# A two-layer float32 backbone kernel: 22 seven-product pairs instead of 20, and sums made by accumulating transfers

## The chip, the core and the metric

The kernel runs on one core of a Trainium2 chip. The metric is the device time of one execution in microseconds (us). Five engines work side by side, each through its own list of instructions in order: PE (TensorE, matmuls), DVE (VectorE), ACT (ScalarE), POOL (GpSimd) and SP (SyncE). They wait for each other by semaphores. SP and POOL issue the transfers between the chip's memory (HBM) and the on-chip memory (SBUF); PE writes its sums to PSUM, which has eight banks of 512 columns.

## The reference

Two layers over 256 latent tokens and 256 context tokens, 1024 channels, all in float32. Each layer is a feed-forward, a mixer (attention, gated convolution, pooling) and a second feed-forward. Only the latent tokens are returned, so the last feed-forward works on them alone, and three feed-forwards work on 512 tokens.

```python
D_MODEL, SEQ, CTX_LEN, D_FF, N_MOD = 1024, 256, 256, 2816, 9
def _swiglu(x, w_gu, w_down):
    g, u = jnp.split(x @ w_gu, 2, axis=-1)
    return (jax.nn.silu(g) * u) @ w_down
...
for l in range(DEPTH):
    mod = (silu_c @ w_mod[l] + b_mod[l]).reshape(B, N_MOD, D_MODEL)
    mod_c = (silu_cc @ w_mod[l] + b_mod[l]).reshape(1, N_MOD, D_MODEL)
    h = h + 0.5 * m[2][:, None] * _swiglu(_modulate(_rms(h, norm_w[l, 0]), m[0], m[1]), ...)
    hc = hc + 0.5 * mc[2][:, None] * _swiglu(...)
    y, yc = _hybrid_mixer(u, uc, ctx_out, w_in[l], w_out[l], ...)
    h = h + m[5][:, None] * y
    h = h + 0.5 * m[8][:, None] * _swiglu(...)
    if ctx_out:
        hc = ...
return h
```

## The kernel before, in words

Activations lie with channels on the 128 partitions and the 512 tokens (latent, context) along the columns: `h` is [128, 8 chunks, 512]. Weights come as a stream of 320 blocks of 128 x 1024 numbers (512 KB) through a ring `raw` of five slots. SP loads block n once PE has finished block n-5.

**Products in three parts.** To keep float32 accuracy, each number is split into a high part (rounded to the fast format) and a low part (the rest). ACT makes `whi` (the high part of a block, line 546), DVE makes `wlo` (the block minus `whi`, line 980). The activations have `xh` and `xl` in the same way, and the hidden values `ah` and `al`. A product is three matmuls: high weight by high x, high weight by low x, low weight by high x (lines 1699 to 1701). An ordinary block is 8 chunks of 3 matmuls of 512 columns.

**A feed-forward** has 22 pairs of blocks (gate and up, pair j writes 128 hidden channels to `hid`) and 22 blocks of the down projection. At pair j, PE waits for the hidden product of pair j-2. ACT applies silu to the gate, DVE multiplies (`hidden`, line 1011). The feed-forwards are numbered f = 0 (layer 0, first), 1 (layer 0, second), 2 (layer 1, first) and 3 (the last, of another form).

**Seven-product pairs.** For the pairs in `SEVENS[f]`, the gate and up blocks are taken as a 2 x 2 matrix of halves and multiplied with the halves of x by the Winograd form of Strassen's scheme: seven products of half size (4 chunks, 3 matmuls each, 256 columns: 84 matmuls) instead of eight (48 matmuls of 512 columns). It needs four sums of halves of x, made once per feed-forward (`x_whole`, `x_sums`, `x_sums_low`: from `xh + xl` = `x32`, which lies in `hid`, to `t32`, then `thi` and `tlo`), and three sums of halves of the weights per pair (`weight_sums` to `s32`, then `shi` and `slo`). One of the seven products needs up-half + gate-half itself, which DVE writes in place into the up block in `raw` (line 1067), before ACT splits that block. PE's third product waits for all of `tlo`, its fifth for `slo`. DVE combines the products (`seven_begin`, `seven_end`, `seven_mul`).

**Modulation.** `modc` = c times `w_mod`, for latent and context. DVE makes it in between: a "pair" is one load of 512 KB into `wm` and two multiply-and-sum operations of 1024 columns, one per stream (`mod_pair`, line 998). There are 36 units of four pairs. POOL loads `wm`, two buffers in turn, one load after each `wm_used` (line 501). How many pairs DVE makes in which step is set by two tables: `MODS_GU[f]` (by pair of blocks) and `MODS_DN[f]` (by block of the down projection); `UNIT_AT[f]` is the first unit and their number.

**The order** of each engine's work is what the loops of `ffn` on DVE, ACT and PE write out; nothing is reordered later. In DVE's loop a step j makes, in this order: splits for pair j+2, or sums and splits of the next seven-product pair; work on x; modulation pairs; the hidden product of j; more splits. `seven(f, j)` decides the branch.

Of the kernel before, what the change touches and what calls it, by code (L numbers as in the profile page):

```python
# [26 lines left out]
P = 128  # L27
D = 1024
DC = D // P
# [53 lines left out]
MODS_GU = ({2: 1, 3: 1, 4: 2, 5: 2, 7: 2, 8: 2, 9: 2, 11: 2, 12: 2, 13: 2, 15: 2, 16: 2, 17: 2, 19: 2, 20: 2, 21: 1},  # L83
           {1: 1, 2: 1, 3: 1, 5: 2, 7: 2, 9: 2, 11: 2, 13: 2, 15: 2, 17: 2, 19: 2, 20: 2, 21: 1},
           {1: 1, 2: 1, 3: 1, 5: 2, 7: 2, 9: 2, 11: 2, 13: 2, 15: 2, 17: 2, 19: 2, 20: 2, 21: 1})
MODS_DN = ({b: 1 for b in range(18)} | {12: 2}, {b: 1 for b in range(18)} | {12: 2, 13: 2, 14: 2, 15: 2},
           {b: 1 for b in range(14)})
HALVES_AT = {20: (0, 1), 21: (2, 3, 4)}
# [27 lines left out]
def program(nc, wstream, wmod, cols, x_t, out):  # L116
    with ExitStack() as ctx:
# [208 lines left out]
        xn_lo = sem("xn_lo")  # L326
        x_sum = sem("x_sum")
        tsum_done = sem("tsum_done")
        thi_done = sem("thi_done")
        tlo_done = sem("tlo_done")  # L330
        wsum_done = sem("wsum_done")
# [8 lines left out]
        silu_a = sem("silu_a")  # L340
# [94 lines left out]

        def seventh(f, j):
            return sum(len(SEVENS[i]) for i in range(f)) + SEVENS[f].index(j)
# [51 lines left out]
        @block.gpsimd  # L489
        def _(pool):  # L490
            u0 = START_UNITS * PAIRS
            pool.wait_ge(wm0_in[DC - 1], 16)
            for c in range(2):
                pool.dma_start(wm[:, c, :, :].rearrange("p a n -> p (a n)"), wmod[u0 + c]).then_inc(wm_in[c], 16)

            def loads(a, b):
                with pool.Fori(a, b) as i:
                    for c in range(2):

                        pool.wait_ge(wm_used, i * 2 + (c - 1 - u0))  # L500
                        pool.dma_start(wm[:, c, :, :].rearrange("p a n -> p (a n)"),  # L501
                                       wmod[bass.ds(i * 2 + c, 1)].rearrange("a p n -> p (a n)"))\
                            .then_inc(wm_in[c], 16)
# [23 lines left out]
            after_mix = (LATE_UNIT + 1) * PAIRS // 2 + 1  # L527
            loads(u0 // 2 + 1, after_mix)
            zeros(0)
            conv_pool_low(0)  # L530
            loads(after_mix, UNITS * PAIRS // 2)
            zeros(1)
            conv_pool_low(1)
# [3 lines left out]
        def _(act):  # L537
# [38 lines left out]
            def weight_sums_high(f, j, n):  # L576

                k = seventh(f, j)
                split(n)
                act.wait_ge(wsum_done, 4 * k + 2)  # L580
                split(n + 1)
                act.wait_ge(wsum_done, 4 * k + 4)
                act.activation(shi[:, :, :, :].rearrange("p k c n -> p (k c n)"),
                               s32[:, :, :].rearrange("p k n -> p (k n)"), ACT.Copy).then_inc(shi_done, 1)

            def silu_seven(f, j):

# [3 lines left out]
                act.activation(ups[:, 0:S], ps[:, 7, 0:S], ACT.Copy).then_inc(s1_done, 1)  # L591
                act.wait_ge(gate_a, k + 1)
                act.activation(sil[:, j % 2, 0:S], first_up[:, 0:S], ACT.Silu).then_inc(silu_a, 1)  # L593
                act.wait_ge(gate_b, k + 1)
                act.activation(sil[:, j % 2, S:T], first_up[:, S:T], ACT.Silu).then_inc(silu_done, 1)

            def ffn(l, st):
# [4 lines left out]
                for j in range(FC):  # L602
# [11 lines left out]
                    if j == 3:  # L614
                        x_sums_high()
                    for c in HALVES_AT.get(j, ()):
# [351 lines left out]
        def _(dve):  # L968
            steps = [0]
# [18 lines left out]
            def mod_pair(u, p, junk=products):  # L988
# [6 lines left out]
                for v in range(2):  # L995
# [3 lines left out]
                                             accum_out=flat[:, at:at + 1]).then_inc(mod_acc, 1)  # L999
# [24 lines left out]
            def x_whole():  # L1024

                for c in range(0, DC, 2):
                    dve.tensor_tensor(x32[:, c:c + 2, :, :, :].rearrange("p c s h t -> p (c s h t)"),
                                      xh32[:, c:c + 2, :].rearrange("p c t -> p (c t)"),
                                      xl[:, c:c + 2, :].bitcast(F32).rearrange("p c t -> p (c t)"), ALU.add)\
                        .then_inc(x_sum, 1)  # L1030

            def x_sums(g):
# [8 lines left out]
                dve.wait_ge(x_sum, 4 * g + 4)  # L1041
# [15 lines left out]
            def weight_sums(f, j, n):  # L1057
# [4 lines left out]
                dve.wait_ge(raw_in[(n + 1) % RING], 16 * ((n + 1) // RING + 1))  # L1062
                if k:
                    dve.wait_ge(products43, k)
                h = KQ * P
                dve.tensor_tensor(s32[:, 0, :], up[:, 0:h], up[:, h:2 * h], ALU.add).then_inc(wsum_done, 1)
# [34 lines left out]
            def seven_end(f, j):  # L1101
# [6 lines left out]
                dve.tensor_tensor(pair_of(ups), twice(two_ups[:, 0:S]), last, ALU.add).then_inc(ups_done, 1)  # L1108

            def seven_mul(f, j):  # L1110
# [3 lines left out]
                halves = hid[:, j * T:(j + 1) * T].rearrange("p (s h t) -> p s h t", s=2, h=2)  # L1114
                for i in range(2):
                    if i:
                        dve.wait_ge(silu_done, FC * f + j + 1)
                    else:
                        dve.wait_ge(silu_a, k + 1)
                    ins = dve.scalar_tensor_tensor(halves[:, :, i, :],  # L1120
                                                   ups[:, i * S:(i + 1) * S].rearrange("p (s t) -> p s t", s=2), -1.0,
                                                   sil[:, j % 2, i * S:(i + 1) * S].rearrange("p (s t) -> p s t", s=2),
                                                   ALU.mult, ALU.mult)
                ins.then_inc(mul_done, 1)
# [113 lines left out]
            def ffn(l, st):  # L1238
# [13 lines left out]
                for j in range(FC):  # L1252
# [14 lines left out]
                    if j == 3:  # L1267
                        x_sums_low(f)
                    for c in HALVES_AT.get(j, ()):
# [1059 lines left out]
```

## Time and profile before

| | |
|---|---|
| time, median of three runs | 1630.32 us (1627.26 to 1631.6) |
| profiled execution | 1629.36 us, of which the span of instructions is 1627.7 |
| PE busy | 1612.9 us (99%), mean granted clock 0.999 |
| DVE busy | 1272.3 us (78%) |
| ACT busy | 690.1 us (42%) |
| POOL busy | 84.7 us (5%) |
| moved by transfers | 250.46 MB, mean 154 GB/s |

The profile is one execution with a row per instruction. A row's idle time stands before it, with what ended it behind an arrow. Matmuls overlap: each row's duration includes its pipeline's depth, so the distance from start to start is the price of one, and a PE that shows as busy may still be spaced out. "Granted clock" is the share of TensorE's full clock.

### The profile page before, as it was taken

What the parts mean: (1) busy time and instruction counts of PE and PEld (TensorE: products, weight loads), DVE (VectorE), ACT (ScalarE), POOL (GpSimd) and SP (SyncE); (2) the same over time, 40 slices, a digit from 0 to 9 for tenths busy, and PEclk for the clock granted to TensorE, in tenths of its full rate; (3) what the DMA queues carried; (4) which work ended last, traced back from release to release, by engine and by line L of the source; (5) the groups of instructions that cost most, each with busy time, mean ns of one, the idle gap of its engine ahead of it and who ended that gap; (6) DMA issues with size and microseconds to landing.
All of it is one profiled execution on the core that took longest, in us unless ns stands there. A gap on an engine that the chain in (4) does not pass through costs nothing.

```text
span 1627.7 us, 24207 instructions
## 1 busy us (share of the span) xinstructions
PE 1612.9 (99%) x9396; PEld 1404.6 (86%) x9396; DVE 1272.3 (78%) x1973; ACT 690.1 (42%) x1056; POOL 84.7 (5%) x149
## 2 busy tenths in 40 slices
PE   8999999999999999999999899999999999999999
PEld 4888888889878898999888798999888997999888
DVE  5887777887878679888878889888888487877654
ACT  5422233324856453333343153333333275665542
POOL 0000000110000100000000100000000000100000
PEclk9999999999999999999999999999999999999999
DMA  9454455563321224444455634444455232365554
GB/s 380 148 191 172 168 174 163 195 200 100 113 67 52 79 97 155 150 147 151 155 176 187 206 105 160 150 147 149 155 179 182 95 114 83 103 201 188 183 187 149
DMA packets 69613, 250.46 MB, mean 154 GB/s; under 512 B 7552, under 2 KB 8576, under 8 KB 69376
## 3 DMA queue, kind: packets, MB, share of 16 engines
q1 hardware_dynamic: 51072, 181.84, 33.3%
q0 software_dynamic: 18432, 67.12, 12.8%
q8 instruction: 74, 1.21, 0.3%
q14 instruction: 35, 0.29, 0.1%
HBM read 247.88 MB, written 1.05 MB: 153 GB/s over the span
## 4 chain that ended last, share of the span: by engine, by line
PE 92%; DVE 5%; DMA 2%; issue 1%; ACT 1%; DVEq 0%; POOLq 0%; ACTq 0%
PE ps L1699 27%; PE ps L1700 26%; PE ps L1701 26%; PE ps L1742 3%; PE ps L1790 2%; PE ps L1743 2%; DMA wm<-wmod 1%; PE ps L1792 1%; PE ps L2108 1%; PE ps L1851 1%; PE ps L2076 1%; DVE shared_b L998 1%; DVE wm L998 1%; DVE wlo L980 1%; PE ps L2090 0%
## 5 line engine op out<-in xcount | busy, mean ns | idle before, releaser
L980 DVE TENSOR_TENSOR wlo<-raw,whi 128x1024 fp32r<-128x1024 f32 x320 | 387.5, 1223 | 191.7 <-ACT whi L546 188.9
L1699 PE MATMUL ps<-xh,whi 128*128 128x512 f32 (+1 forms) x1420 | 497.1, 350 | 2.7 <-DVE xl L1185 2.3
L1700 PE MATMUL ps<-xl,whi 128*128 128x512 f32 (+1 forms) x1420 | 489.1, 344 | 0.0
L1701 PE MATMUL ps<-xh,wlo 128*128 128x512 f32 (+1 forms) x1420 | 488.8, 344 | 0.0
L546 ACT ACTIVATE whi<-raw 128x1024 fp32r<-128x1024 f32 x320 | 335.6, 1056 | 354.6 <-PE ps L1701 269.1
L1699 PEld LDWEIGHTS ps<-xh,whi 128*128 128x128 f32 x1420 | 268.7, 189 | 41.2 <-DVE xl L1185 4.4
L1701 PEld LDWEIGHTS ps<-xh,wlo 128*128 128x128 f32 x1420 | 268.7, 189 | 32.6
L1700 PEld LDWEIGHTS ps<-xl,whi 128*128 128x128 f32 x1420 | 268.9, 189 | 32.3 <-issue 0.7
L1700 PE MATMUL ps<-al,whi 128*128 128x512 f32 (+2 forms) x768 | 263.8, 343 | 0.0
L1699 PE MATMUL ps<-ah,whi 128*128 128x512 f32 (+1 forms) x668 | 236.2, 354 | 4.7 <-DVE wlo L980 2.8
L1701 PE MATMUL ps<-ah,wlo 128*128 128x512 f32 (+1 forms) x668 | 235.5, 353 | 0.0
L1700 PEld LDWEIGHTS ps<-al,whi 128*128 128x128 f32 x768 | 146.3, 190 | 17.1
L998 DVE SCALAR_TENSOR_TENSOR wm<-wm,cb 128x1024 f32<-128x1024 f32 x128 | 156.1, 1220 | 0.0
L1699 PEld LDWEIGHTS ps<-ah,whi 128*128 128x128 f32 x668 | 126.9, 190 | 23.1 <-DVE wlo L980 3.0
L1701 PEld LDWEIGHTS ps<-ah,wlo 128*128 128x128 f32 x668 | 126.9, 190 | 16.9
L501 POOL DMA_DIRECT2D wm<-wmod x126 | 66.6, 529 | 983.6 <-DVEq L1001 959.0
L559 ACT ACTIVATE shared_b<-ps 128x512 f32<-128x512 f32 x46 | 27.5, 599 | 208.8 <-PE ps L1701 208.7
L998 DVE SCALAR_TENSOR_TENSOR shared_a<-wm,cb 128x1024 f32<-128x1024 f32 x73 | 89.1, 1221 | 10.2 <-DMA wm<-wmod 5.7
L1011 DVE TENSOR_TENSOR hid<-shared_b,ps 128x512 f32<-128x512 f32 x46 | 31.6, 687 | 69.5 <-ACT shared_b L559 66.7
L998 DVE SCALAR_TENSOR_TENSOR shared_b<-wm,cb 128x1024 f32<-128x1024 f32 x55 | 67.0, 1219 | 8.8 <-DMA wm<-wmod 8.7
L1742 PE MATMUL ps<-xh,whi 128*128 128x512 f32 x208 | 73.5, 399 | 0.0
L593 ACT ACTIVATE shared_b<-shared_b 128x256 f32<-128x256 f32 x20 | 8.4, 419 | 137.5 <-DVE shared_b L1094 137.5
(217 smaller groups left out, 2295.6 us busy)
## 6 DMA issues: line engine op xcount, KB each, us to landing
raw<-wstream SPq DMA_DIRECT2D x320, 512.0 KB, 3.5
wm<-wmod POOLq DMA_DIRECT2D x128, 512.0 KB, 4.8
wm<-wmod SPq DMA_DIRECT2D x8, 1024.0 KB, 16.8
h<-x_t SPq DMA_DIRECT2D x4, 512.0 KB, 6.4
cb<-cols SPq DMA_DIRECT2D x1, 1024.0 KB, 19.7
out_t<-h SPq DMA_DIRECT2D x8, 128.0 KB, 2.6
K<-cols SPq DMA_DIRECT2D x1, 907.0 KB, 19.9
K<-cols SPq DMA_DIRECT2D x1, 265.5 KB, 2.9
```

The lines of the kernel that those rows point to most:

```text
L501: pool.dma_start(wm[:, c, :, :].rearrange("p a n -> p (a n)"), wmod[bass.ds(i * 2 + c, 1)].rearrange("a p n -> p (a n)"))\
L546: act.activation(whi[:, n % SPL, :, :].rearrange("p a b -> p (a b)"), raw[:, n % RING, :], ACT.Copy)\
L559: act.activation(sil[:, j % 2, 0:w], ps[:, gu_bank(f, 2 * j), 0:w], ACT.Silu).then_inc(silu_done, 1)
L980: dve.tensor_tensor(wlo[:, n % RING, :, :].rearrange("p a b -> p (a b)"), raw[:, n % RING, :], whi[:, n % SPL, :, :].rearrange("p a b -> p ...
L998: dve.scalar_tensor_tensor(rows if v else junk, rows, 1.0, cb[:, v, :], ALU.mult, ALU.mult, accum_out=flat[:, at:at + 1]).then_inc(mod_acc, 1)
L1011: dve.tensor_tensor(hid[:, j * T:j * T + w], sil[:, j % 2, 0:w], ps[:, gu_bank(f, 2 * j + 1), 0:w], ALU.mult).then_inc(mul_done, 1)
L1699: pe.matmul(out_ap, hi_w, hi_x, start=start, stop=False)
L1700: pe.matmul(out_ap, hi_w, lo_x, start=False, stop=False)
L1701: return pe.matmul(out_ap, lo_w, hi_x, start=False, stop=stop)
L1742: pe.matmul(ps[:, bank, :], whi[:, n % SPL, c, :], xh[:, c, :], start=c == 0, stop=False)
L1743: return pe.matmul(ps[:, bank, 0:S], wlo[:, n % RING, c, :], xh[:, c, 0:S], start=False, stop=c == DC - 1)
L1790: pe.matmul(ps[:, banks[d], 0:2 * w], hi_w, pair.rearrange("p v t -> p (v t)"), start=start, stop=False)
```

## The change

- `SEVENS`: in feed-forwards 1 and 2 the seven-product pairs are now the even ones from 4 to 20 (nine each) instead of the odd ones from 5 to 19 (eight each). Feed-forward 0 keeps its four.
- Whole x: DVE's four additions go. POOL copies `xh` into `x32` with two transfers of 1 MB (SBUF to SBUF), waits for both, and adds `xl` to it with two accumulating transfers (`accum_op`). DVE's `x_sums` stands at step 4 of feed-forward 0 and step 2 of the others, and waits for `x_sum`.
- Weight sums in feed-forwards 1 and 2: POOL adds half of the gate block from HBM onto the up block in `raw` (256 KB, accumulating, `third_sum`); DVE then makes three sums instead of four. DVE's sums and ACT's split of that block wait for `third_in`.
- `seven_mul`: one operation of 512 columns instead of two of 256; ACT's silu writes its halves in the order of the tokens.
- Modulation: from unit 28 on (`X_ONLY`) only the latent stream's operation is made, the context's columns are set to zero once. The pairs are dealt anew: 48, 36 and 44 in feed-forwards 0 to 2 instead of 48, 44 and 36.
- POOL's loads are written out in order, between the other transfers, instead of a loop.
- `HALVES_AT`: in feed-forwards 1 and 2 the first five hidden splits all stand at step 21.

```diff
-UNIT_AT = {0: (4, 12), 1: (16, 11), 2: (27, 9)}
+UNIT_AT = {0: (4, 12), 1: (16, 9), 2: (25, 11)}
+X_ONLY = 28
+X_SUMS_AT = (4, 2, 2)
+ACCUMULATED = (1, 2)
-SEVENS = ((7, 11, 15, 19), (5, 7, 9, 11, 13, 15, 17, 19), (5, 7, 9, 11, 13, 15, 17, 19))
+SEVENS = ((7, 11, 15, 19),
+          (4, 6, 8, 10, 12, 14, 16, 18, 20),
+          (4, 6, 8, 10, 12, 14, 16, 18, 20))
...
-MODS_DN = ({b: 1 for b in range(18)} | {12: 2}, {b: 1 for b in range(18)} | {12: 2, 13: 2, 14: 2, 15: 2},
-           {b: 1 for b in range(14)})
...
+             {21: (0, 1, 2, 3, 4)},
...
+            def whole_x(f):
+
+                if f == 0:
+                    pool.wait_ge(mul_done, 1)
+                pool.wait_ge(xl_done, XT[(0, 2, 3)[f]] + 2 * DC)
+                for c in (0, KQ):
+                    pool.dma_start(x32[:, c:c + KQ, :, :, :].rearrange("p c s h t -> p (c s h t)"),
+                                   xh32[:, c:c + KQ, :].rearrange("p c t -> p (c t)")).then_inc(x_copy, 16)
+                pool.wait_ge(x_copy, 32 * (f + 1))
+                for c in (0, KQ):
+                    pool.dma_start(x32[:, c:c + KQ, :, :, :].rearrange("p c s h t -> p (c s h t)"),
+                                   xl[:, c:c + KQ, :].bitcast(F32).rearrange("p c t -> p (c t)"), accum_op=ALU.add)\
+                        .then_inc(x_sum, 16)
+
+            def third_sum(f, j):
+
+                n = first_block(f) + 2 * j + 1
+                pool.wait_ge(raw_in[n % RING], 16 * (n // RING + 1))
+                pool.dma_start(raw[:, n % RING, 0:KQ * P], wstream[n - 1][:, 0:KQ * P], accum_op=ALU.add)\
+                    .then_inc(third_in, 16)
+
+            def ffn(f, m0):
+
+                made = m0
+                if f:
+                    whole_x(f)
+                for j in range(FC):
+                    if f == 0 and j == 1:
+                        whole_x(f)
+                    made += MODS_GU[f].get(j, 0)
+                    loads_to(u0 + 2 + made)
+                    if f in ACCUMULATED and seven(f, j + 2):
+                        third_sum(f, j + 2)
+                loads_to(u0 + 2 + made + sum(MODS_DN[f].values()))
+                return made + sum(MODS_DN[f].values())
...
-                act.wait_ge(wsum_done, 4 * k + 2)
+                if f in ACCUMULATED:
+                    act.wait_ge(third_in, 16 * (k - before_accumulated + 1))
+                else:
+                    act.wait_ge(wsum_done, 4 * k + 2)
...
-                    if j == 3:
+                    if j == X_SUMS_AT[f] + 1:
                         x_sums_high()
...
-                for v in range(2):
+                for v in range(2 if u < X_ONLY else 1):
...
-            def x_whole():
-
-                for c in range(0, DC, 2):
-                    dve.tensor_tensor(x32[:, c:c + 2, :, :, :].rearrange("p c s h t -> p (c s h t)"),
...
-                dve.wait_ge(x_sum, 4 * g + 4)
+                dve.wait_ge(x_sum, 32 * (g + 1))
...
+                if f in ACCUMULATED:
+                    dve.tensor_tensor(s32[:, 1, :], up[:, 0:h], up[:, h:2 * h], ALU.add).then_inc(wsum_done, 2)
+                    dve.wait_ge(wsum_done, 4 * k + 2)
+                    dve.tensor_tensor(s32[:, 0, :], s32[:, 1, :], gate[:, 0:h], ALU.subtract).then_inc(wsum_done, 1)
+                    dve.tensor_tensor(s32[:, 2, :], s32[:, 1, :], gate[:, h:2 * h], ALU.add).then_inc(wsum_done, 1)
+                    return
...
-                    if j == 1:
-                        x_whole()
-                    if j == 2:
+                    if j == X_SUMS_AT[f]:
                         x_sums(f)
```

How the instructions move. DVE, start of feed-forward 1, before, from the first hidden products on (`t<-hid` are the token sums, `tlo<-t,thi` their low parts, `s<-raw` the first weight sum, `wm,modc` a modulation operation):

```order
L1042 TENSOR_TENSOR t<-hid 128x1024 [waits x_sum]
L1043 TENSOR_TENSOR t<-hid 128x1024
L1045 SCALAR_TENSOR_TENSOR t<-t,hid 128x1024 [waits tsum_done]
L1048 SCALAR_TENSOR_TENSOR t<-t,hid 128x1024 [waits tsum_done]
L998 SCALAR_TENSOR_TENSOR shared_a,modc<-wm,cb 128x1024 [waits wm_in1]
L998 SCALAR_TENSOR_TENSOR wm,modc<-wm,cb 128x1024
L1011 TENSOR_TENSOR hid<-shared_b,ps 128x512 [waits mod_acc,silu_done]
L980 TENSOR_TENSOR wlo<-raw,whi 128x1024 [waits hi_done]
L1054 TENSOR_TENSOR tlo<-t,thi 128x1024 [waits thi_done] x4
```

and after:

```order
L1093 TENSOR_TENSOR t<-hid 128x1024 [waits x_sum]
L1094 TENSOR_TENSOR t<-hid 128x1024
L1096 SCALAR_TENSOR_TENSOR t<-t,hid 128x1024 [waits tsum_done]
L1099 SCALAR_TENSOR_TENSOR t<-t,hid 128x1024 [waits tsum_done]
L1070 TENSOR_TENSOR hid<-shared_b,ps 128x512 [waits silu_done]
L1121 TENSOR_TENSOR s<-raw 128x512 [waits third_in,products43,raw_in2]
L1123 TENSOR_TENSOR s<-s,raw 128x512 [waits wsum_done]
L1124 TENSOR_TENSOR s<-s,raw 128x512
L1038 TENSOR_TENSOR wlo<-raw,whi 128x1024 [waits hi_done,wsum_done]
L1038 TENSOR_TENSOR wlo<-raw,whi 128x1024 [waits hi_done]
L1136 TENSOR_TENSOR slo<-s,shi 128x1536 [waits shi_done]
L1105 TENSOR_TENSOR tlo<-t,thi 128x1024 [waits thi_done] x4
```

The modulation operations have gone from here, and the weight sums of the first seven-product pair now stand between the token sums and their low parts, a pair earlier than before.

POOL at the same place, after (before, only loads of `wm` stood here, each waiting for `wm_used`); `hid<-xh` and `hid<-xl` are the transfers of whole x, `raw<-wstream` the third sums:

```order
L526 DMA hid<-xh 128x2048 [waits xl_done]
L526 DMA hid<-xh 128x2048
L530 DMA hid<-xl 128x2048 [waits x_copy]
L530 DMA hid<-xl 128x2048
L538 DMA raw<-wstream 128x512 [waits raw_in3]
L538 DMA raw<-wstream 128x512 [waits raw_in2]
L517 DMA wm<-wmod 128x1024 [waits wm_used] x2
L538 DMA raw<-wstream 128x512 [waits raw_in1]
```

The third sum of the first seven-product pair stands behind all four transfers of whole x in POOL's list.

## Rows read from the trace of the kernel before

**Rows 1.** The page, busy time of each engine.
```profile
PE 1612.9 (99%) x9396; PEld 1404.6 (86%) x9396; DVE 1272.3 (78%) x1973; ACT 690.1 (42%) x1056; POOL 84.7 (5%) x149
```
**Rows 2.** Waits of PE: total us, times, longest.
```profile
PE ps L1699 <- DVE wlo L980: 3.0, 2, 2.8
PE ps L1699 <- DVE xl L1185: 2.3, 4, 0.6
PE ps L1699 <- DVE h L1135: 1.9, 1, 1.9
```
**Rows 3.** Timeline of PE, pairs 4 and 5, feed-forward 1: start, duration, instruction.
```profile
629.98 0.39 PE L1699 MATMUL ps<-xh,whi 128*128 128x512 f32 x1
...
640.86 0.28 PE L1699 MATMUL ps<-xh,whi 128*128 128x256 f32 x1
...
650.93 0.40 PE L1699 MATMUL ps<-xh,whi 128*128 128x512 f32 x1
```
**Rows 4.** Timeline of PE, end of feed-forward 1; idle in brackets.
```profile
923.13 0.28 PE L1701 MATMUL ps<-ah,wlo 128*128 128x256 f32 x1
926.20 0.39 PE L1699 MATMUL ps<-ah,whi 128*128 128x256 f32 x1 [2.79 <-DVE wlo L980]
...
933.42 0.28 PE L1701 MATMUL ps<-ah,wlo 128*128 128x256 f32 x1
935.62 0.39 PE L1699 MATMUL ps<-ah,whi 128*128 128x256 f32 x1 [1.92 <-DVE h L1135]
```
**Rows 5.** Busy by window: PE, PEld, DVE, ACT, POOL; clock, DMA share, GB/s.
```profile
927.00:935.00 8.00, 6.70 (x44) 6.50 (x42) 7.71 (x17) 0.00 (x0) 1.06 (x2) 0.79 0.42 144
```
**Rows 6.** Timeline of DVE, end of feed-forward 1, two splits in succession.
```profile
917.37 1.23 DVE L980 TENSOR_TENSOR wlo<-raw,whi 128x1024 fp32r<-128x1024 f32 x1
...
924.92 1.23 DVE L980 TENSOR_TENSOR wlo<-raw,whi 128x1024 fp32r<-128x1024 f32 x1
```
**Rows 7.** Timeline of DVE, start of feed-forward 1.
```profile
597.08 1.27 DVE L1185 SCALAR_TENSOR_TENSOR xl<-shared_b,modc,xh 128x256 fp32r<-128x256 f32 x3
...
616.70 1.22 DVE L1042 TENSOR_TENSOR t<-hid 128x1024 f32<-128x1024 f32 x1
...
620.23 1.23 DVE L1048 SCALAR_TENSOR_TENSOR t<-t,hid 128x1024 f32<-128x1024 f32 x1
...
625.63 4.62 DVE L1054 TENSOR_TENSOR tlo<-t,thi 128x1024 fp32r<-128x1024 f32 x4
...
635.94 2.36 DVE L980 TENSOR_TENSOR wlo<-raw,whi 128x1024 fp32r<-128x1024 f32 x2
638.22 1.75 DVE L1076 TENSOR_TENSOR slo<-s,shi 128x1536 fp32r<-128x1536 f32 x1
```
**Rows 8.** Timeline of DVE, feed-forward 0, hidden products of pairs 0 and 3.
```profile
50.11 0.69 DVE L1011 TENSOR_TENSOR hid<-shared_b,ps 128x512 f32<-128x512 f32 x1 [0.68 <-ACT shared_b L559]
...
81.85 0.69 DVE L1011 TENSOR_TENSOR hid<-shared_b,ps 128x512 f32<-128x512 f32 x1
```
**Rows 9.** Landings of `raw`, of `wm`; transfers, 0:40 (two rows), then 598:618.
```profile
DMA to landing us min/median/max: 3.3/3.5/18.2
...
DMA to landing us min/median/max: 3.6/4.8/19.3
...
GB/s 0 19 212 364 363 356 326 348 412 428 410 426 410 418 422 410 401 414 414 410 401 414 414 410 401 410 422 406 406 397 418 401 406 418 439 396 388 403 438 389
...
q1 hardware_dynamic: 4469, 15.03, 96.3%
...
q1 hardware_dynamic: 720, 2.62, 37.7%
```
**Rows 10.** Groups of DVE by form: busy us, mean ns, idle before.
```profile
L998 DVE SCALAR_TENSOR_TENSOR wm<-wm,cb 128x1024 f32<-128x1024 f32 x128 | 156.1, 1220 | 0.0
L1011 DVE TENSOR_TENSOR hid<-shared_b,ps 128x512 f32<-128x512 f32 x46 | 31.6, 687 | 69.5 <-ACT shared_b L559 66.7
L1066 DVE TENSOR_TENSOR s<-raw 128x512 f32<-128x512 f32 x20 | 13.7, 684 | 0.0
```

More of the change, by code:

```diff
@@ L330, in program @@
         tlo_done = sem("tlo_done")
+        third_in = sem("third_in")
         wsum_done = sem("wsum_done")
@@ L434, in seven, with first_block @@
             return f < 3 and j in SEVENS[f]
+        before_accumulated = sum(len(SEVENS[f]) for f in range(DEPTH + 1) if f not in ACCUMULATED)
+        def first_block(f):
+            return (0, FFN + MIX, PER_LAYER)[f]
         def seventh(f, j):
@@ L494, in _ @@
                 pool.dma_start(wm[:, c, :, :].rearrange("p a n -> p (a n)"), wmod[u0 + c]).then_inc(wm_in[c], 16)
[L496 to L503, printed above, removed]
+            at = [u0 + 2]
@@ new lines, in loads_to @@
+            def loads_to(end):
+                while at[0] < min(end, UNITS * PAIRS):
+                    q = at[0]
+                    pool.wait_ge(wm_used, q - 1 - u0)
+                    pool.dma_start(wm[:, q % 2, :, :].rearrange("p a n -> p (a n)"), wmod[q]).then_inc(wm_in[q % 2], 16)
+                    at[0] += 1
+            def whole_x(f):
[10 more added lines that the diff above has]
+                        .then_inc(x_sum, 16)
@@ L524, in conv_pool_low @@
                         .then_inc(cl_done, 1)
-            after_mix = (LATE_UNIT + 1) * PAIRS // 2 + 1
-            loads(u0 // 2 + 1, after_mix)
+            m1 = ffn(0, 0)
             zeros(0)
             conv_pool_low(0)
-            loads(after_mix, UNITS * PAIRS // 2)
+            m2 = ffn(1, m1)
+            ffn(2, m2)
             zeros(1)
@@ L591, in silu_seven @@
                 act.activation(ups[:, 0:S], ps[:, 7, 0:S], ACT.Copy).then_inc(s1_done, 1)
+                halves = sil[:, j % 2, :].rearrange("p (s h t) -> p s h t", s=2, h=2)
+                gates = first_up.rearrange("p (h s t) -> p h s t", h=2, s=2)
                 act.wait_ge(gate_a, k + 1)
[L593 removed]
+                act.activation(halves[:, :, 0, :], gates[:, 0, :, :], ACT.Silu)
                 act.wait_ge(gate_b, k + 1)
[L595 removed]
+                act.activation(halves[:, :, 1, :], gates[:, 1, :, :], ACT.Silu).then_inc(silu_done, 1)
             def ffn(l, st):
@@ L613, in ffn @@
                         weight_sums_high(f, j + 1, n + 2)
-                    if j == 3:
+                    if j == X_SUMS_AT[f] + 1:
                         x_sums_high()
-                    for c in HALVES_AT.get(j, ()):
+                    for c in HALVES_AT[f].get(j, ()):
                         hidden_high(f, c)
@@ L1061, in weight_sums @@
                 dve.wait_ge(raw_in[n % RING], 16 * (n // RING + 1))
-                dve.wait_ge(raw_in[(n + 1) % RING], 16 * ((n + 1) // RING + 1))
+                if f in ACCUMULATED:
+                    dve.wait_ge(third_in, 16 * (k - before_accumulated + 1))
+                else:
+                    dve.wait_ge(raw_in[(n + 1) % RING], 16 * ((n + 1) // RING + 1))
                 if k:
@@ L1107, in seven_end @@
                 dve.tensor_tensor(first_up[:, S:T], two_ups[:, S:T], ps[:, 5, S:T], ALU.add).then_inc(gate_b, 1)
-                dve.tensor_tensor(pair_of(ups), twice(two_ups[:, 0:S]), last, ALU.add).then_inc(ups_done, 1)
+                dve.tensor_tensor(ups.rearrange("p (s h t) -> p h s t", s=2, h=2),
+                                  twice(two_ups[:, 0:S]).rearrange("p h (s t) -> p h s t", s=2),
+                                  last.rearrange("p h (s t) -> p h s t", s=2), ALU.add).then_inc(ups_done, 1)
             def seven_mul(f, j):
@@ L1113, in seven_mul @@
                 dve.wait_ge(ups_done, k + 1)
[L1114 to L1124, printed above, removed]
+                dve.wait_ge(silu_done, FC * f + j + 1)
+                dve.scalar_tensor_tensor(hid[:, j * T:(j + 1) * T], ups, -1.0, sil[:, j % 2, :], ALU.mult, ALU.mult)                    .then_inc(mul_done, 1)
             def gate_columns(m):
@@ L1262, in ffn @@
                         weight_sums_low(f, j + 1)
-                    if j == 1:
-                        x_whole()
-                    if j == 2:
+                    if j == X_SUMS_AT[f]:
                         x_sums(f)
-                    if j == 3:
+                    if j == X_SUMS_AT[f] + 1:
                         x_sums_low(f)
-                    for c in HALVES_AT.get(j, ()):
+                    for c in HALVES_AT[f].get(j, ()):
                         hidden_low(f, c)
```

20 lines of the change are left out of this document (12 added, 8 removed).

## The prediction

> **What bounds the kernel now.** I read the busy shares first: PE is busy for 1612.9 of 1627.7 us, DVE for 1272.3 [rows 1]. Next the waits of PE: behind the opening they are a handful: two for wlo, the longest 2.8 us, one of 1.9 us for h, and four for xl of at most 0.6 us [rows 2]. So the time is PE's own matmuls, one behind the other. DVE work that is removed is worth nothing in itself; it counts only where PE waits for it. The other direction is open: DVE and the transfers have little room, and whatever makes PE wait is added in full.
>
> The timeline of PE gives the prices. An ordinary pair of blocks runs from 629.98 to 640.86 us, 10.88 us; a seven-product pair from 640.86 to 650.93, 10.07 us [rows 3].
>
> The only stretch where PE loses anything of size is the end of the second feed-forward (number 1; the first is number 0, the third number 2). PE starts a matmul at 923.13, the next at 926.20 (the distance is otherwise 0.12 us: 2.95 lost), then one at 933.42 and the next at 935.62 (2.08 lost) [rows 4]. Between them the granted clock was 0.79 over 8 us: behind the first wait PE ran for a while at the lower of its two levels (1.2 instead of 2.4 GHz), 0.21 x 8 = 1.7 us more [rows 5]. DVE explains it: between two splits it has two modulation pairs of 2 x 1.22 us each and a wait for their rows (split at 917.37, next split only at 924.92) [rows 6]; the update of h then starts late.
>
> **The change part by part.** The sum is made against the profiled execution, 1629.36 us (its span 1627.7 and 1.66 around it); the median of the runs is 1630.32, 1 us above.
>
> *22 instead of 20 seven-product pairs.* Two ordinary pairs become seven-product ones: 2 x (10.88 - 10.07) = -1.6 us, on the path, since PE is saturated [rows 3].
>
> *The modulation work dealt anew, and halved from unit 28 on.* Before, the second feed-forward makes 44 pairs, four of them as seconds in blocks 12 to 15 of its down projection; now 36, one per block. In the first feed-forward, whose down projection keeps one per block with one second, PE doesn't wait, so with fewer than that the two waits above should go: 2.95 + 2.08 and the clock's 1.7: -6.7 us. The third feed-forward gets 44 pairs, but 32 of them have one operation of 1.22 us instead of two [rows 10]: DVE saves 32 x 1.22 = 39 us there, all beside PE's matmuls and so worth 0. What the others lose in DVE time is also worth 0.
>
> *The sums of a pair by an accumulating transfer.* On DVE 3 operations of 0.68 us instead of 4 in 18 pairs [rows 10], one multiplication instead of two: about 12 us of DVE, hidden, worth 0. It adds a wait: DVE's sums and ACT's split of the second block wait for third_in, behind which the splits of the next pairs are queued. The up block of pair j+2 is asked for when the gate block of pair j is done, 2.9 us into the pair, and lands 3.5 us later [rows 9]; POOL then issues 256 KB. The nearest row is POOL's 512 KB load, 3.6 to 4.8 us to landing [rows 9]. So it is there 10 to 11 us into pair j, and DVE wants it at about 11, when PE has ended pair j. Where POOL first stands at a load's wait for DVE, 1 to 2 us more. Bounds 0 and 2 us per pair of DVE time; what stands behind it has more room than that (DVE ended slo at 638.22 + 1.75 = 640.0 [rows 7], and PE needed it only four products or 48 matmuls of 0.12 us into the pair of 640.86, at 646.6), so PE pays 0 in both bounds. I take 0.
>
> *Whole x by transfers.* DVE loses four additions of 1024 columns, of the length of its token sums (1.22 us), in each of three feed-forwards: 4.9 us each time, hidden, 0. In their place POOL waits for the last xl, copies 2 x 1 MB of high parts from SBUF to SBUF, waits until both have landed, and adds 2 x 1 MB of low parts. DVE's token sums wait for that at pair 2. This is what decides.
>
> What DVE has to do from there on, in the second feed-forward: four token sums (616.70 to 620.23 + 1.23, 4.8 us), one hidden product 0.7, three weight sums of 0.68, 2.0, two splits 2.3 (635.94 to 638.22), slo 1.7 and four tlo 4.6 [rows 7, 10]: 16.1 us; starts lie a little closer than ends, so I take 15.8. PE now has its first seven-product pair at pair 4, which starts at 629.98 as the ordinary one did [rows 3], and wants all of tlo for its third product, 24 matmuls of 0.12 us later: 632.9. So whole x has to be there at 632.9 - 15.8 = 617.1. Before, the first such pair was pair 5; the distance shrinks by a pair. In front of the token sums DVE has only two splits and two hidden products left, so it stands ready for them well before.
>
> The last xl ends at 597.08 + 1.27 = 598.35 [rows 7]. A POOL load of 512 KB lands after 3.6 us at best, and at the 410 GB/s that the queues moved at the start its bytes take 1.3: 2.3 us are fixed [rows 9]. The copy is 2.1 MB, 5.1 us. Meanwhile block loads run (2.62 MB in 598 to 618 us, five of them) [rows 9]; two, 1.05 MB, 2.6 us, fall into the copy. It lands at 598.35 + 2.3 + 5.1 + 2.6 = 608.4. The accumulating part has no row. Its bounds: each byte counts once, 2.3 + 5.1 + one load 1.3, landing at 617.1; or the engines have to fetch the destination as well as the source, which a sum needs, so twice the bytes: 2.3 + 10.2 + two loads 2.6, landing at 623.5. I take the second, because the engines were 96% busy at the start at some 410 GB/s [rows 9], so bytes are what they are limited by, and both operands have to pass.
>
> The Trainium skill says on this, in "Collectives: The Full Stack", section "The bandwidth ceiling: the fold count and why AG ≠ RS ≠ AR", that an adding transfer isn't slowed by the addition but needs two source reads on one ring, and so goes at about half of a copy's rate. No row here shows one; by that rule the sum would be the one of the second bound, by the rows of plain loads alone the first.
>
> Landing at 623.5, PE waits 6.4 us in pair 4; after the wait of [rows 4] it ran slow at a price of 1.7 [rows 5], so 8.1 in all. The third feed-forward runs the same instructions over the same pairs: another 8.1. The first has its token sums at pair 4: the copy starts behind the hidden product of 50.11, and DVE comes to them behind that of 81.85, 31.7 us later [rows 8], against 25.2 that the transfers take: 0. So +16.2.
>
> Sum: 1629.36 - 1.6 - 6.7 + 16.2 = 1637.3. With some of the wait taken up by DVE's slack (its order leaves no more than a us), I say 1636.
>
> **Rivals.**
> First: the accumulation goes at a copy's rate. Whole x is there at 617.1, PE doesn't wait, or under 1 us, and what is left is -8.3 to -6.5: 1621 to 1623. For it speaks that no row shows the reading from SBUF, which may run beside the rest; against it, that both operands have to pass. It needs both feed-forwards to land before about 619 (wait under 2 us, no slow clock): the sign turns where the two waits with the clock reach 8.3, that is at a landing of about 620.
> Second: it is slower still (each packet's fetch of the destination follows its write, or POOL's third sum for pair 4, which stands behind 2 MB in the same queue, comes last): landing at 628, waits of 11 and the clock, 2 x 12.6 - 8.3 = +17: 1646.
> Third: between: part of the loads doesn't collide, the landing is 619.5 to 621.5, waits 2.5 to 4.5 with the clock 1 to 1.7 each, and the change comes out even: 1626 to 1633.
> That the waits at 923 us stay (the dealing doesn't relieve DVE there) would add 6.7 to any of these; the first feed-forward speaks against it.
>
> **How the numbers follow.** Accumulation with both operands paid 0.45 (1636; its own range 1631 to 1642), at a copy's rate 0.34 (1621), between 0.12 (1629), slower still 0.09 (1646). About 0.3% (4.9 us) is what a measurement of this kernel can tell from no change. Faster takes the second case and a little of the between: 0.36; within 0.3% the rest of the between and the low end of the first: 0.19; slower 0.45. The range, 1620 to 1646, leaves out the tail of the slowest case and the best of the fast one.
>
> **What would show it.** On PE at pair 4 of the second and third feed-forward an idle of some 6 us before the third product, released by DVE's tlo, and a granted clock under 1 behind it; on DVE a wait for a DMA before the token sums, some 12 us long; accumulating transfers that take about twice the copies. At 923 to 939 no wait of PE over 0.6. Pair lengths of 10.07. If DVE doesn't wait longer than to 618, I am wrong on the accumulation; if PE waits in later pairs for slo or wlo, on the third sums.

## The result and the profile after

The changed kernel takes 1648.89 us (median of four, 1647.34 to 1651.14) against 1629.53 us before in the same session: ratio 1.0119, interval 1.0106 to 1.0132. It is slower by 19 us and 13 us above the 1636 that I forecast, outside my range.

The profiled execution has a span of 1646.1 us, 18.4 more than before. The page, busy time of each engine (answers to [rows 1]):

```profile
PE 1617.6 (98%) x9468; PEld 1411.6 (86%) x9468; DVE 1222.1 (74%) x1878; ACT 692.3 (42%) x1062; POOL 109.5 (7%) x179
```

DVE has 50 us less to do, and the kernel is slower: DVE's load was never the bound. PE's waits in the changed kernel (total us, times, longest; answers to [rows 2]):

```profile
PE ps L1750 <- DVE wlo L1038: 14.4, 7, 3.4
PE ps L1750 <- DVE tlo L1105: 4.6, 2, 2.7
```

and where they are, from the timeline of PE, the start of each matmul with the idle time ahead of it:

```profile
634.76 0.55 PE L1750 MATMUL ps<-xh,whi 128*128 128x256 f32 x1 [3.39 <-DVE wlo L1038]
...
642.10 0.36 PE L1750 MATMUL ps<-thi,whi 128*128 128x256 f32 x1 [1.89 <-DVE tlo L1105]
...
999.21 0.54 PE L1750 MATMUL ps<-xh,whi 128*128 128x256 f32 x1 [3.43 <-DVE wlo L1038]
...
1006.56 0.55 PE L1750 MATMUL ps<-thi,whi 128*128 128x256 f32 x1 [2.73 <-DVE tlo L1105]
...
1134.52 0.36 PE L1750 MATMUL ps<-xh,whi 128*128 128x256 f32 x1 [3.45 <-DVE wlo L1038]
...
1157.81 0.36 PE L1750 MATMUL ps<-xh,whi 128*128 128x256 f32 x1 [0.59 <-DVE wlo L1038]
...
1181.49 0.36 PE L1750 MATMUL ps<-xh,whi 128*128 128x256 f32 x1 [2.46 <-DVE wlo L1038]
```

The first four stand in pair 4 of feed-forwards 1 and 2, the last three at pairs 16, 18 and 20 of feed-forward 2 alone. The two waits at the end of feed-forward 1 [rows 4] have gone.

A reader can do the account by stages: PE waits 0.6 us for the last `xl` at each norm, before and after, so from one such place to the next is one feed-forward with what is around it. The busy view of both stretches (length, then PE, PEld, DVE, ACT, POOL busy, clock, DMA share, GB/s), before:

```profile
593.65:957.91 364.26, 358.79 (x2044) 317.34 (x2044) 303.03 (x451) 128.32 (x173) 23.30 (x44) 1.00 0.49 159
957.91:1315.03 357.12, 356.54 (x2045) 315.70 (x2045) 284.26 (x419) 128.47 (x173) 17.97 (x34) 1.00 0.46 148
```

and after:

```profile
594.88:959.30 364.42, 358.56 (x2081) 319.04 (x2081) 279.76 (x407) 129.81 (x176) 30.02 (x49) 0.99 0.52 166
959.30:1333.72 374.42, 361.19 (x2081) 320.80 (x2081) 262.01 (x375) 129.41 (x176) 33.21 (x55) 0.99 0.54 170
```

The stretch of feed-forward 1 is as long as before (+0.2 us; the experiments show that a loss and a gain cancel there), that of feed-forward 2 is 17.3 us longer. Ahead of both 1.2 us are lost (a wait of 0.80 us in feed-forward 0 among them), behind them nothing.

Pair 4 is what the prediction described. POOL in feed-forward 1, from its timeline:

```profile
599.88 1.12 POOL L526 DMA_DIRECT2D hid<-xh  x2 [54.14 <-DVE xl L1238]
609.39 1.78 POOL L530 DMA_DIRECT2D hid<-xl  x2 [8.39 <-DMA hid<-xh]
625.72 0.87 POOL L538 DMA_DIRECT2D raw<-wstream  x1 [14.55 <-DMA raw<-wstream]
```

and DVE, from its own:

```profile
626.07 1.23 DVE L1093 TENSOR_TENSOR t<-hid 128x1024 f32<-128x1024 f32 x1 [11.46 <-DMA hid<-xl]
```

The copies start at 599.88, the accumulating transfers at 609.39, and DVE gets whole x at 626.07 after idling 11.5 us. Behind the wait PE runs at half clock. The window just behind the matmul of 634.76:

```profile
634.70:639.70 5.00, 4.94 (x23) 4.97 (x24) 5.00 (x5) 5.00 (x7) 0.00 (x0) 0.50 0.00 0
```

The second place is not in the prediction. DVE at the weight sums of feed-forward 2 (timeline):

```profile
1105.15 0.70 DVE L1121 TENSOR_TENSOR s<-raw 128x512 f32<-128x512 f32 x1 [3.54 <-DMA raw<-wstream]
...
1130.62 0.69 DVE L1121 TENSOR_TENSOR s<-raw 128x512 f32<-128x512 f32 x1 [4.86 <-DMA raw<-wstream]
```

and POOL ahead of the second of them:

```profile
1121.14 0.53 POOL L517 DMA_DIRECT2D wm<-wmod  x1 [3.72 <-DVEq L1060]
1123.43 0.53 POOL L517 DMA_DIRECT2D wm<-wmod  x1 [1.76 <-DVEq L1060]
1123.95 0.92 POOL L538 DMA_DIRECT2D raw<-wstream  x1
```

POOL waits for DVE's modulation pairs of the same step (L1060 is their release), issues their two loads, and only then issues the third sum. DVE, which has just released it, comes to the weight sums at 1125.8 and waits 4.9 us for that transfer. DVE's waits for third sums over the kernel (total us, times, longest), then the same in the stretch 1079 to 1190 us alone:

```profile
DVE s L1121 <- DMA raw<-wstream: 40.5, 15, 4.9
```
```profile
DVE s L1121 <- DMA raw<-wstream: 19.6, 5, 4.9
```

The 15 waits sort by what stands ahead of the third sum in the same step of POOL's list. With no load ahead DVE waits for 0 to 2.1 us. With one load (pairs 14, 16 and 18 of feed-forward 1, pairs 10, 12 and 14 of feed-forward 2) it waits 2.8 to 3.5 us, and with two (pairs 16, 18 and 20 of feed-forward 2) 3.8 to 4.9 us. In the stretch 1079 to 1190 us DVE waits only for transfers (4.9 us more for modulation rows) and for its own results, never for PE or ACT: it has no lead left.

The transfers on the page, KB of one and median us from its issue to its landing (the transfers of whole x are issued two at a time):

```profile
hid<-xh POOLq DMA_DIRECT2D x6, 1024.0 KB, 7.3
hid<-xl POOLq DMA_DIRECT2D x6, 1024.0 KB, 12.3
raw<-wstream POOLq DMA_DIRECT2D x18, 256.0 KB, 5.1
```

### The profile page after: what moved, and what is told of

It reads as the page before. It is cut to its first block, busy times and chain, and to the rows that moved or that the text cites. A ratio compares the mean times of both kernels' runs of the same rounds, so it can differ in the third digit from the quotient of the medians.

```text
span 1646.1 us, 23849 instructions
## 1 busy us (share of the span) xinstructions
PE 1617.6 (98%) x9468; PEld 1411.6 (86%) x9468; DVE 1222.1 (74%) x1878; ACT 692.3 (42%) x1062; POOL 109.5 (7%) x179
## 4 chain that ended last, share of the span: by engine, by line
PE 80%; DVE 11%; DMA 7%; issue 1%; ACT 1%; POOL 0%; DVEq 0%; ACTq 0%
PE ps L1750 23%; PE ps L1751 22%; PE ps L1752 22%; DMA raw<-wstream 4%; PE ps L1793 3%; DVE wlo L1038 2%; PE ps L1841 2%; DVE shared_a L1056 2%; PE ps L1794 1%; DMA wm<-wmod 1%; DVE wm L1056 1%; DMA hid<-xl 1%; PE ps L1843 1%; DVE tlo L1105 1%; PE ps L2159 1%
## 5 line engine op out<-in xcount | busy, mean ns | idle before, releaser
L1751 PE MATMUL ps<-xl,whi 128*128 128x512 f32 (+1 forms) x1404 | 484.0, 345 | 0.0
L1752 PE MATMUL ps<-xh,wlo 128*128 128x512 f32 (+1 forms) x1404 | 483.7, 345 | 0.0
L1056 DVE SCALAR_TENSOR_TENSOR wm<-wm,cb 128x1024 f32<-128x1024 f32 x96 | 117.2, 1221 | 0.0
L756 ACT ACTIVATE shared_a<-h 128x256 f32<-128x256 f32 (+1 forms) x64 | 31.4, 496 | 65.3 <-DVE h L1188 63.2
## 6 DMA issues: line engine op xcount, KB each, us to landing
wm<-wmod SPq DMA_DIRECT2D x8, 1024.0 KB, 16.7
hid<-xl POOLq DMA_DIRECT2D x6, 1024.0 KB, 12.3
```

The costliest lines, as they stand in the source:

```text
L756: act.activation(sq[:, d % 2, a:b], h[:, d, a:b], ACT.Square).then_inc(sq_done, 1)
L1056: dve.scalar_tensor_tensor(rows if v else junk, rows, 1.0, cb[:, v, :], ALU.mult, ALU.mult, accum_out=flat[:, at:at + 1])\
L1751: pe.matmul(out_ap, hi_w, lo_x, start=False, stop=False)
L1752: return pe.matmul(out_ap, lo_w, hi_x, start=False, stop=stop)
```

## The experiments

The theory after the first look (A): two separate costs, the late whole x at pair 4 and the late third sums in feed-forward 2, on top of two gains. Rivals: the new dealing overloads DVE (B), or the later waits are an echo of pair 4 (C). The first four kernels ran on one chip.

**Whole x by DVE again.**
```diff
-                if f:
-                    whole_x(f)
...
+                    if j == 1:
+                        x_whole()
```


> The changed kernel with whole x put together by DVE again (its four additions at step 1) and no copies by POOL; everything else as changed. Theory A (two separate costs: whole x lands some 9 us too late for pair 4 of feed-forwards 1 and 2, about 8 and 10 us with the slow clock; and the third sums are issued late in feed-forward 2, about 8 us at pairs 16 to 20): the first cost goes, the second stays: 1629 to 1632 us, no wait of PE at pair 4, the waits at pairs 16 to 20 still there. Theory B (one cost: DVE is overloaded by the new dealing, and the late x only starts it): giving DVE 4.9 us more per feed-forward makes it 1640 or more. Theory C (one cost, all from the transfers of whole x, the later waits being its echo): 1621 to 1623.


Measured: 1631.13 us, ratio 1.0007 (0.9997 to 1.0016). Its two stages:

```profile
593.84:950.17 356.33, 355.75 (x2081) 316.76 (x2081) 284.58 (x411) 130.03 (x176) 27.22 (x45) 1.00 0.48 158
950.17:1315.05 364.88, 358.42 (x2081) 319.12 (x2081) 266.43 (x379) 130.28 (x176) 30.44 (x51) 0.99 0.50 163
```

Feed-forward 1 is 8.1 us shorter than in the changed kernel, with no wait of PE left inside: the late x cost 8.1 us there. Feed-forward 2 keeps one wait of PE of 5.9 us, at 1118.41. So the later waits are no echo (C falls), and DVE having more to do made nothing slower (B falls). I had expected waits at pairs 16 to 20; there is one, at pair 16.

**Third sums on DVE again.**
```diff
-ACCUMULATED = (1, 2)
+ACCUMULATED = ()
```


> The changed kernel with all three weight sums on DVE again (four operations, in place), whole x still by transfers. Theory A: the waits at pairs 16 to 20 of feed-forward 2 go, those at pair 4 stay (8 and about 9 us): 1638 to 1641 us. Theory B (dealing): DVE has 0.7 us more per pair, the later waits stay or grow: 1649 to 1652. Theory C (echo of the late x): as now, 1648.


Measured: 1640.65 us, ratio 1.0069 (1.0049 to 1.0089). Stages:

```profile
593.55:957.99 364.44, 358.57 (x2081) 319.01 (x2081) 284.85 (x416) 129.95 (x176) 21.93 (x40) 0.99 0.47 159
957.99:1323.13 365.14, 359.00 (x2080) 319.55 (x2081) 267.39 (x384) 130.08 (x176) 25.03 (x46) 0.99 0.50 167
```

Feed-forward 1 stays, feed-forward 2 becomes 9.3 us shorter: the third sums cost that, and there only.

**Both undone.** The two edits above together.


> The changed kernel with both kinds of accumulating transfers undone: 22 seven-product pairs, the new dealing and the halved modulation remain. Theory A: only the gains are left, 1.6 for two pairs and 6.7 for the waits at the end of feed-forward 1: 1620 to 1622 us, and at most 1 us of waits inside the feed-forwards. Theory B (DVE is overloaded by the dealing): 1630 or more, with waits at pairs 12 to 20.


Measured: 1620.52 us, ratio 0.9936 (0.9920 to 0.9953). Stages:

```profile
594.42:950.74 356.32, 355.75 (x2081) 316.77 (x2081) 289.46 (x420) 130.26 (x176) 19.06 (x36) 1.00 0.44 151
950.74:1307.05 356.31, 355.74 (x2081) 316.75 (x2081) 271.88 (x388) 130.30 (x176) 22.18 (x42) 1.00 0.47 160
```

Against before, 7.9 and 0.8 us less: one seven-product pair each (0.8), and 7.1 for the end of feed-forward 1. DVE is busier than in the changed kernel by 10 us per stage, and PE doesn't wait.

**The third sum ahead of the loads in POOL's list.**
```diff
+                    if f in ACCUMULATED and seven(f, j + 2):
+                        third_sum(f, j + 2)
                     made += MODS_GU[f].get(j, 0)
                     loads_to(u0 + 2 + made)
-                    if f in ACCUMULATED and seven(f, j + 2):
-                        third_sum(f, j + 2)
```


> The changed kernel with one exchange in POOL's list: in each step the third sum stands in front of the loads of modulation rows, which wait for DVE. Theory A, in the form that the third sums are late because POOL stands at a load's wait: the waits at pairs 16 to 20 go, those at pair 4 stay: 1639 to 1642 us, and DVE's waits for the third sums fall from 40 us to under 15. Rival: they are late because such a transfer itself takes 5 us behind a block load: DVE's waits stay above 30 us and the time within 2 us of 1648.9.


Measured: 1641.36 us, ratio 1.0067 (1.0051 to 1.0084). DVE's waits for third sums:

```profile
DVE s L1121 <- DMA raw<-wstream: 16.3, 15, 2.0
```

They fall from 40.5 to 16.3 us (I had expected under 15), and the waits of PE at pairs 16 to 20 go. The same transfers, issued ahead of the loads of their step, take 0.7 us more than no such transfers at all (1641.36 against 1640.65), which is inside both intervals.

**A plain copy in place of the accumulating one** (the high parts are left out of the sums).
```diff
-                                   xl[:, c:c + KQ, :].bitcast(F32).rearrange("p c t -> p (c t)"), accum_op=ALU.add)\
+                                   xl[:, c:c + KQ, :].bitcast(F32).rearrange("p c t -> p (c t)"))\
```


> The changed kernel with the two accumulating transfers of whole x turned into plain copies of the same size, places and waits; the addition of x's high parts is left out of the token sums, so the output is not the reference's. Theory A (an accumulating transfer pays for both operands, 12.3 us against 7.3): the second pair of transfers takes about as long as the first, whole x lands 5 us sooner, 20 to 21 us behind the last xl; the waits at pair 4 shrink to 1 to 3 us each, the later ones stay: 1634 to 1639 us. Rival (the second pair is slow because block loads and third sums run beside it): it still takes over 11 us and the time stays above 1645.


Measured: 1640.31 us, ratio 1.0072 (1.0051 to 1.0094), just outside what I expected. The transfers:

```profile
hid<-xh POOLq DMA_DIRECT2D x6, 1024.0 KB, 7.3
hid<-xl POOLq DMA_DIRECT2D x6, 1024.0 KB, 7.8
```

The median of one transfer falls from 12.3 to 7.8 us. The two of feed-forward 1 together take 10.2 us from the first issue to the last landing, where the accumulating ones take 16.7: the accumulation costs 6.4 us per two transfers. Whole x is there at 619.57 instead of 626.07, yet only 3.5 us of the 8.1 come back in feed-forward 1 (it lasts 360.9 us). A wait of PE of 2.9 us for `tlo` stays, and behind it the granted clock is 0.68 over 5.4 us: 2.9 and 1.7 for the clock make the 4.6 that are left. DVE and POOL there:

```profile
620.74 0.89 POOL L538 DMA_DIRECT2D raw<-wstream  x1 [10.37 <-DMA raw<-wstream]
...
625.88 0.70 DVE L1121 TENSOR_TENSOR s<-raw 128x512 f32<-128x512 f32 x1 [0.95 <-DMA raw<-wstream]
```

Now the third sum of pair 4 is awaited too: it waits for its block, and DVE waits 0.95 us for it. The rest of the 2.9 is whole x, still somewhat late. Feed-forward 2 has two waits at the third sums here, of 3.9 and 4.4 us.

**First seven-product pair at pair 6.**
```diff
-          (4, 6, 8, 10, 12, 14, 16, 18, 20),
+          (6, 8, 10, 12, 14, 16, 18, 20),
```
(twice)


> The changed kernel with the first seven-product pair of feed-forwards 1 and 2 at pair 6 instead of 4 (20 such pairs in all), everything else as changed, whole x and third sums by transfers. Theory A (whole x misses a deadline that pair 4 sets): the deadline moves by 21 us, the waits at pair 4 go; 1.6 us for two pairs come back; the late third sums stay: 1648.9 - 17 + 1.6 = 1632 to 1635 us. Rival (the transfers of whole x delay the block loads, and that stops PE wherever the first such pair stands): above 1640, with waits of PE for wlo of blocks in pairs 3 to 5.


Measured: 1636.83 us, ratio 1.0052 (1.0032 to 1.0072), 2 us above the expected stretch. Stages:

```profile
594.77:951.87 357.10, 356.52 (x2045) 315.67 (x2045) 273.98 (x399) 128.23 (x173) 29.29 (x48) 1.00 0.52 168
951.87:1322.12 370.25, 361.23 (x2044) 319.50 (x2044) 256.35 (x367) 128.18 (x173) 32.43 (x54) 0.99 0.53 171
```

Feed-forward 1 is as fast as with 20 pairs and no transfers: the copies, the accumulations and the slower block loads beside them cost PE nothing when nobody needs whole x by pair 4. Feed-forward 2 pays 13 us for late third sums, 4 more than the changed kernel. Its first late pair is again pair 16; why it pays more was not tried.

**Whole x by DVE, third sums early.** The edits of the first and the fourth together.


> Whole x by DVE, and the third sums by accumulating transfers but in front of the modulation loads in POOL's list. If the third sums cost only through their place in that list, this is as fast as with all sums on DVE: 1620 to 1622 us. If the transfers cost by themselves (5 us to landing, DVE waiting for each), PE still waits at pairs 16 to 20: 1625 to 1630.


Measured: 1620.67 us, ratio 0.9950 (0.9933 to 0.9967), equal to both undone, though DVE still waits for them:

```profile
DVE s L1125 <- DMA raw<-wstream: 21.0, 18, 2.8
```

So the third sums save DVE time and bring nothing, and cost nothing when issued in time.

**Old places of the pairs, new dealing.** `SEVENS` as before on top of both undone.


> Both kinds of accumulating transfers undone, and the seven-product pairs of feed-forwards 1 and 2 at the old odd places (20 in all), with the new dealing of the modulation. By the timeline's prices (10.88 against 10.07 us a pair) it takes 1.6 us more than the same kernel with 22 pairs, 1620.5 before: 1621.5 to 1623. If the even places cost or save more than the pairs themselves (another lead of DVE at pair 4, the first hidden splits at step 21), the difference is below 0.5 or above 3 us.


Measured: 1623.29 us, ratio 0.9962 (0.9949 to 0.9974). That is 0.3 us above the expected stretch. Its stages last 357.10 and 357.12 us, against 356.32 and 356.31: 0.8 us per pair, as the prices of [rows 3] say; the medians, from different chips, differ by 2.8.

**Old dealing, new places.** `MODS_GU`, `MODS_DN` and `UNIT_AT` as before on top of both undone.


> Both kinds of accumulating transfers undone, 22 seven-product pairs at the new places, but the modulation dealt by the old tables (44 pairs in feed-forward 1, four of them as seconds in its down projection), still halved from unit 28 on. If the gain of the fast variant (1620.5 us) comes from the dealing at the end of feed-forward 1, it loses 6.7 us: 1626 to 1629, with PE's waits of about 2.8 and 1.9 us there again. If it comes from DVE's smaller load in general, the waits stay away: 1621 to 1622.


Measured: 1635.99 us, ratio 1.0034 (1.0022 to 1.0046), 7 us above the expected stretch. PE's waits:

```profile
PE ps L1755 <- DVE tlo L1108: 3.9, 2, 2.2
...
PE ps L1755 <- DVE wlo L1033: 3.6, 4, 2.0
PE ps L1755 <- DVE h L1191: 2.6, 1, 2.6
```

The waits at the end of feed-forward 1 are there, as expected. What I left out: the old tables put modulation into steps 1 to 3, ahead of `tlo`, and with the first pair at 4 that makes PE wait for `tlo` in both feed-forwards. The new dealing is worth 15 us to this set of pairs (the stages are 11.4 and 3.9 us longer than with both undone), not 6.7.

**Whole x by transfers alone**, on the old pairs and the old dealing.


> The kernel before (20 pairs at the old places, old dealing, all weight sums on DVE) with only whole x by POOL's transfers, and the halved modulation, which takes DVE time in feed-forward 2 alone. Theory (whole x comes 25 us behind the last xl, and the first seven-product pair sets the deadline): with pair 5 first there are 10.9 us more, but DVE has three modulation pairs of 2.4 us in steps 1 to 3, so about 3 us of waiting remain in each of feed-forwards 1 and 2, with the slow clock 4 to 5: 1636 to 1640. If the transfers cost by disturbing others wherever the pairs stand: above 1643; if pair 5 is late enough: 1629 to 1631.


Measured: 1643.00 us, ratio 1.0087 (1.0072 to 1.0103), which only the case of disturbed loads comes near. Yet PE's waits are not for disturbed loads. PE in pair 4 of feed-forward 1:

```profile
635.64 0.50 PE L1747 MATMUL ps<-xh,whi 128*128 128x512 f32 x1 [2.54 <-DVE hid L1067]
```

It waits for the hidden product of pair 2, which DVE has queued behind its wait for x (token sums only from 627.71, hidden product at 634.90). A deadline that I had not looked at is earlier than `tlo` here. Its stages cost 6.5 and 4.2 us. Of the 6.5, some 1.1 stand at the end of feed-forward 1, where the wait of [rows 4] has grown from 2.79 to 3.93 us. Another 3.0 us lie ahead, in feed-forward 0: PE waits 1.9 us at pair 7, and the granted clock behind it is 0.70 over 5.6 us. The run with third sums on DVE has the same instructions up to there and waits 0.80 us, at full clock. So the same instructions can take either time, and the run does not show that this part comes from the transfers.

**Two steps on.** On top of both undone, the token sums of feed-forward 0 back at step 2:
```diff
-X_SUMS_AT = (4, 2, 2)
+X_SUMS_AT = (2, 2, 2)
```


> The fast variant (22 pairs, new dealing, all sums on DVE) with the token sums of feed-forward 0 at step 2 again instead of 4. PE's wait of 0.8 us for wlo at pair 7 there, which every variant with step 4 shows, goes: 1 us less than 1620.5, so 1619 to 1620. If that wait comes from elsewhere, no change.


Measured: 1619.45 us, ratio 0.9937 (0.9924 to 0.9951); the wait of 0.8 us at pair 7 is gone, as expected. And with pairs 9, 13 and 17 of feed-forward 0 as seven-product pairs too:
```diff
-SEVENS = ((7, 11, 15, 19),
+SEVENS = ((7, 9, 11, 13, 15, 17, 19),
```


> The same with three more seven-product pairs, 9, 13 and 17 in feed-forward 0 (25 in all). By PE's prices 3 x 0.8 = 2.4 us less: 1617 us. But DVE has 6 modulation pairs in each four steps there, 40 us of work in 42: if it falls behind, PE waits for wlo and the time is 1620 to 1628.


Measured: 1617.03 us (1616.82 to 1617.39), ratio 0.9924 (0.9910 to 0.9937): the best version, 12 us faster than before and 32 faster than the changed kernel, without an accumulating transfer. DVE was able to do the work: PE's waits there are those of the opening and of the norms.

## Why the prediction was right and wrong

**The sign and the first cost: right.** I gave 8.1 us for whole x in feed-forward 1; whole x by DVE gives back 8.1. Whole x landed at 626.07, 26.5 us behind the last `xl` (599.6), where I had 25.2. The pieces hold: copy and accumulation, a deadline set by pair 4, a wait of PE for DVE, a slow clock. That the sum agrees to a tenth is luck, though, because two misses cancel. Whole x came 1.3 us later than I had it, so the third product starts 8.0 us late and not 6.4 (it stands 47.2 us behind the start of the stage, against 39.2 with both undone). And the clock adds almost nothing to that, where I had 1.7: most of the wait stands at the start of pair 4 (3.39 us for `wlo`, since the splits also come behind the token sums), and the half clock behind it runs while PE would have waited for `tlo` anyway (1.89 us are left of that wait).

**The accumulation pays for both operands: right, as far as shown.** Taking off the 2.3 us that I called fixed, (16.7 - 2.3) to (10.2 - 2.3) is 1.8, and the medians of one transfer give the same. The packets of the two accumulating transfers occupied the 16 DMA engines for 63.2% of the 16 us from 610 to 626; those of the plain copies, as many and as large, for 53.2% of the 9.5 us from 610 to 619.5: twice the time for the same 2.10 MB. The Trainium skill says in "Collectives: The Full Stack", section "The bandwidth ceiling: the fold count and why AG ≠ RS ≠ AR", of the adding step of a collective that the add needs two source reads per chunk, and gives about half of a copy's rate. The trace agrees in the time (1.8 and 2), but it shows the time only, not the reads.

**The gains: right.** 0.8 us per pair, and 7.1 at the end of feed-forward 1, where I had 6.7.

**The step that failed: "so PE pays 0 in both bounds. I take 0", for the third sums.** Measured: 9.3 us, all in feed-forward 2 (third sums undone, 374.42 to 365.14). The step had two errors. My bound for DVE's wait per pair was 2 us; it holds only where no load stands ahead of the third sum (0 to 2.1 us). It is 2.8 to 3.5 us behind one load and 3.8 to 4.9 us behind two, and the transfer itself takes 5.1 us in the median, where I had 3.6 to 4.8. And I compared one delay with the room of one `slo`, while each delay is passed on to the next period: DVE's lead shrinks until a split is late, at pair 16, and from 1079 to 1190 us DVE never waits for PE or ACT (with both kinds of transfers undone it waits 8.7 us for them in the matching stretch, 1071 to 1175). POOL's list has the third sums of steps 14 to 18 behind two loads that wait for DVE; I had read that order and not priced it. That the place in the list is the cause is shown: with the third sums ahead of the loads the 9.3 us are gone but for 0.7. That feed-forward 1 pays nothing fits with its three such delays of 2.8 to 3.2 us, where feed-forward 2 has six in a row, but this was not tried apart.

**A smaller miss:** whole x cost 8.8 us in feed-forward 2 (third sums undone, 365.14 to 356.31), not 8.1, and about 1 us in feed-forward 0, which I had at 0: its token sums at step 4 crowd two modulation pairs. It is the step and not the transfers, since every variant with step 4 shows this wait, also with DVE's additions.

**The range** held the cases of the accumulation but none in which a second place adds to it. The sum was 1637.3, of which I took off 1.3 for a slack of DVE that did not show; with the missing 9.3, 0.7 and about 1 it makes 1648, against 1648.1 of the profiled execution. My slower rival, 1646, comes near in number only: it wanted whole x 29.7 us behind the last `xl`, and it was 26.5.

**The account by stages.** Feed-forward 0 costs 1.2 us. Feed-forward 1 costs 8.1 for whole x and gains 7.1 and 0.8. Feed-forward 2 costs 9.3 and 8.8 and gains 0.8. With 0.3 gained behind them this is 18.4, the difference of the spans. The two costs in feed-forward 2 aren't quite separate: undone in the other order, whole x gives back 9.5 and the third sums 8.6.

## What to carry to other kernels

Work taken from an engine that isn't the bound brings nothing, and the latency of what replaces it is paid if a queue stands still for it: here the two kinds of accumulating transfers took 24 of the 50 us off DVE and made the kernel 28 us slower (1648.89 against 1620.52). Without them and with all else of the change, it is 9 us faster than before. An issuing queue is in order too: put a transfer that is needed soon ahead of those that wait for somebody. And when a delay recurs each period, compare it with the slack of a period, not with the lead at one place.

## What the runs showed of the hardware

- Two accumulating transfers of 1 MB each within SBUF, issued together, had landed 16.7 us behind the first issue, where the same two without accumulation took 10.2 (medians of one: 12.3 and 7.8).
- Block loads suffer beside such transfers: 512 KB from issue to landing took 3.4 us (median) before and 8.0 after, in the stretch of the copies and accumulations. It is not the accumulation: with plain copies in its place the median is 7.7 (597 to 620 us). Views of transfers in 597 to 618 us before, then 597 to 625 after:

```profile
raw<-wstream SPq DMA_DIRECT2D x5, 512.0 KB, 3.4
```
```profile
raw<-wstream SPq DMA_DIRECT2D x6, 512.0 KB, 8.0
```

- A wait of PE of 3.39 us was followed by 5 us at half clock (window above), while waits of 0.6 and 0.8 us were not followed by a lower clock. In between, the length of the wait alone does not tell: behind waits of 1.89 and 2.46 us in the changed kernel (at 642.10 and 1181.49) the granted clock was 1.00, behind one of 1.92 us (whole x by transfers alone, at 109.38) 0.70 over 5.6 us, and behind one of 2.90 us (plain copy, at 636.65) 0.68 over 5.4 us.
